# A decoder step's projection rewritten: token shift finished inside it, wider column chunks, zeros stored in seven pieces

## What is computed

```python
xn   = rmsnorm(x, g_mix)                       # x: 1088 rows of 1024
proj = xn @ w_in                               # 1024 x 3328
ret_p, rw_p = proj[..., :1536], proj[..., 1536:]
# token shift on the 1792 RWKV columns
prev = concatenate([s_shift, rw_p[:-1]])       # the row before; zeros / state_shift in front
rw_s = rw_p + (prev - rw_p) * rwkv_mu
s_shift_new = rw_p[:, -1]
```

## Time and profile before

| | before |
|---|---|
| median of three runs | 2183.63 us |
| the profiled execution | 2183.41 us, its span 2181.6 us |
| PE busy | 1847.1 us, 85% |
| DVE busy | 1217.1 us, 56% |
| ACT busy | 835.4 us, 38% |
| POOL busy | 305.9 us, 14% |
| projection, to the first instruction of the mixers | 0 to 365.0 us |
| mixers, to the first transfer of the attention | 365.0 to 885.1 us |

### The profile page before, as it was taken

The page is one execution under the profiler, slowest core; times in us unless marked ns, Lnnn a source line. Parts: engine busy times, 40 slices in busy tenths (PEclk is TensorE's granted clock), DMA queues, the critical chain, the costliest instruction groups (busy, mean ns, idle before and its releaser), DMA issues. The chain is left out here.

```text
span 2181.6 us, 36329 instructions
## 1 busy us (share of the span) xinstructions
PE 1847.1 (85%) x15218; PEld 1559.4 (71%) x15218; DVE 1217.1 (56%) x1285; ACT 835.4 (38%) x923; POOL 305.9 (14%) x262
## 2 busy tenths in 40 slices
PE   5999996687788879589999999854999999999940
PEld 5999996566666667478788888333888888888830
DVE  5200100776788876542333332127899999999926
ACT  4211210332333331340221212003777777777723
POOL 1000000322333323100000000001111111111003
PEclk9999998897999998799999999876999999999975
DMA  4422213417311120855201113526999999999928
GB/s 159 145 79 79 79 49 134 125 60 185 98 65 70 70 62 14 287 213 197 102 29 51 39 59 152 196 85 234 371 404 402 404 403 402 403 402 403 356 102 308
DMA packets 110630, 407.76 MB, mean 187 GB/s; under 512 B 25176, under 2 KB 47960, under 8 KB 82352
## 3 DMA queue, kind: packets, MB, share of 16 engines
q1 hardware_dynamic: 86000, 344.32, 42.6%
q10 hardware_dynamic: 17440, 36.00, 4.4%
q0 software_dynamic: 7072, 25.69, 3.0%
HBM read 345.91 MB, written 68.53 MB: 190 GB/s over the span
## 5 line engine op out<-in xcount | busy, mean ns | idle before, releaser
L2361 DVE TENSOR_TENSOR ex_w_lo<-moe_raw,ex_w_hi 128x2048 fp32r<-128x2048 f32 x192 | 431.2, 2285 | 67.0 <-ACT ex_w_hi L2426 66.9
L2426 ACT CAST ex_w_hi<-moe_raw 128x2048 fp32r<-128x2048 f32 x192 | 364.1, 1913 | 133.3 <-PE banks L2271 90.3
L2271 PE MATMUL banks<-ex_w_hi,ex_x_hi 128*128 128x512 f32 x512 | 208.0, 406 | 10.9 <-issue 6.4
L295 PE MATMUL banks<-pj_w_hi,pj_x_lo 128*128 128x416 f32 x576 | 203.7, 354 | 0.0
L295 PE MATMUL banks<-pj_w_hi,pj_x_hi 128*128 128x416 f32 x576 | 203.3, 353 | 0.1
L2271 PE MATMUL banks<-ex_w_hi,ex_x_lo 128*128 128x512 f32 x512 | 202.1, 395 | 0.0
L2271 PE MATMUL banks<-ex_w_lo,ex_x_hi 128*128 128x512 f32 x512 | 201.5, 394 | 0.0
L295 PE MATMUL banks<-pj_w_lo,pj_x_hi 128*128 128x416 f32 x576 | 201.5, 350 | 0.0
L199 DVE TENSOR_TENSOR pj_w_lo<-pj_w,pj_w_hi 128x3328 fp32r<-128x3328 f32 x8 | 29.0, 3623 | 221.6 <-ACT pj_w_hi L254 221.6
L247 ACT COPY pj_out<-banks 128x416 f32<-128x416 f32 x72 | 36.4, 506 | 253.7 <-PE banks L295 253.7
L2271 PEld LDWEIGHTS banks<-ex_w_hi,ex_x_hi 128*128 128x128 f32 x512 | 97.5, 190 | 42.9 <-issue 21.9
(11 more groups left out here) (375 smaller groups left out, 3823.4 us busy)
## 6 DMA issues: line engine op xcount, KB each, us to landing
moe_raw<-w_e_gate SPq DMA_DIRECT2D x64, 1024.0 KB, 7.7
moe_raw<-w_e_up SPq DMA_DIRECT2D x64, 1024.0 KB, 7.4
moe_raw<-w_e_down SPq DMA_DIRECT2D x64, 1024.0 KB, 7.4
blocks<-ex_y ACTq DMA_DIRECT2D x32, 512.0 KB, 7.7
proj<-pj_out ACTq DMA_DIRECT2D x72, 208.0 KB, 1.9
pj_w<-w_in SPq DMA_DIRECT2D x8, 1664.0 KB, 8.7
mx_pin<-proj SPq DMA_DIRECT2D x8, 1664.0 KB, 7.0
h<-at_h SPq DMA_DIRECT2D x18, 512.0 KB, 2.6
```

The source lines that it names most:

```text
L295: ins = pe.matmul(PS[:, 4 + t % BUFS, 0:W], a[:, t, k, :], b[:, par, k, :], start=k == 0 and n == 0, stop=k == KC - 1 and n == len(pairs) - 1)
L2271: ins = pe.matmul(out, a, b, start=first and i == 0, stop=final and i == 2)
L2361: v.tensor_tensor(w_lo[:, j], raw[:, j], as_f32(w_hi[:, j]), ALU.subtract).then_inc(S_("w_split"), 1)
L2426: act.copy(w_hi[:, j], raw[:, j]).then_inc(S_("w_high"), 1)
```

## The change

- **Inputs laid out on the host.** x comes turned as well (`xT`), w_in in column chunks whose every piece is one contiguous run in each partition, g_mix, state_shift and mu in the shapes of their tiles. No arithmetic moves to the host.
- **Projection.** 7 chunks instead of 8: four of 448 columns (the RWKV part, done first) and three of 512. The row norm is no longer applied to x but to the result, where PSUM is emptied; the gain g goes into the split of the weights. No PE transposes. The sample tile's low parts lie in the 64 unused columns of its high part, so it takes two matmuls a block instead of three. Banks go round over all eight.
- **Token shift in the projection.** For the RWKV chunks DVE writes from PSUM p = rstd·mu·(xW) to `pm` and rstd·(xW) − p to `out`; SP stores `pm` to DRAM one row down (`put`), reads the rows of the same tile back (`bring`), POOL adds them to `out`, SP stores that to `proj`. The new shift states are stored from here. 
- **Mixers.** No `prev`, no mu, no shift operations, no state_shift rows; `keys` and `key_sum` move forward on DVE; `load(j)` does not wait for r's shift; `lora_act` waits for the load.
- **Zeros.** Instead of 8 MB once, 2, 2, 2, 3, 2, 2 and 3 blocks of 512 KB, each behind the load of pairs 0 to 6.

The core of the diff:

```diff
+    CHUNKS = [(NRET + 448 * c, 448) for c in range(4)] + [(512 * c, 512) for c in range(3)]
+    NCH = len(CHUNKS)
+    shifted = lambda c: CHUNKS[c][0] >= NRET
+    W, HALF, BUFS, MB = 512, KC // 2, 5, 3
...
+                def load_w(c, h):
+                    i, n = 2 * c + h, HALF * CHUNKS[c][1]
+                    if i >= 3:
+                        sp.wait_ge(S_("w_split"), HALF * (i - 2))
+                    sp.dma_start(piece(c, h), d["w_in"][:, w_at[c] + h * n:w_at[c] + (h + 1) * n]).then_inc(S_(f"w_loaded{i % 3}"), 16)
...
+                def put(c, t):
+                    m, (col, n) = moved(c, t), CHUNKS[c]
+                    b, r = m % MB, rows_of(t)
+                    cols = slice(col - NRET, col - NRET + n)
+                    sp.wait_ge(S_("dve_evicted"), dve_evicted(c, t))
+                    sp.dma_start(d["pm"][t * P + 1:t * P + 1 + r, cols], pm[0:r, b, 0:n]).then_inc(S_(f"put{b}"), 16)
...
+                def bring(c, t):
+                    m, (col, n) = moved(c, t), CHUNKS[c]
+                    b, r = m % MB, rows_of(t)
+                    to, cols = S_(f"up{b}"), slice(col - NRET, col - NRET + n)
+                    sp.wait_ge(S_(f"put{b}"), 16 * (m // MB + 1))
+                    if m >= MB:
+                        sp.wait_ge(S_("added"), m - MB + 1)
+                    sp.dma_start(up[0:r, b, 0:n], d["pm"][t * P:t * P + r, cols]).then_inc(to, 16)
+                    if t == NT:
...
+                steps = [(c, t) for c in range(NCH) for t in range(TILES)]
+                for n in range(len(steps) + 2):
+                    if n < len(steps):
+                        c, t = steps[n]
+                        if t == 0 and 1 <= c < NCH - 1:
+                            load_w(c + 1, 0)
+                            load_w(c + 1, 1)
+                        if shifted(c):
+                            put(c, t)
+                    if 1 <= n <= N_SH * TILES:
+                        bring(*steps[n - 1])
+                    if n >= 2:
+                        store(*steps[n - 2])
...
+                def shares(c, t, src, cols):
+                    r, m, n = rows_of(t), moved(c, t), number(c, t)
+                    rstd, width = st[0:r, t, 2:3], CHUNKS[c][1]
+                    b = m % MB
+                    if m >= MB:
+                        v.wait_ge(S_(f"put{b}"), 16 * (m // MB))
+                    lk(v.scalar_tensor_tensor(pm[0:r, b, 0:width], src, rstd, mu[0:r, cols], ALU.mult, ALU.mult))
+                    if t >= NT - 1:
+                        q = slice(P - 32, P) if t < NT else slice(0, NS)
+                        if moved(c, t) > NT:
+                            v.wait_ge(S_("raw_stored"), 32 * (m // TILES))
+                        v.tensor_scalar(raw[q, 0:width], src[q], st[q, t, 2:3], None, ALU.mult)
+                    out_free(v, c, t)
+                    v.scalar_tensor_tensor(out[0:r, n % BUFS, 0:width], src, rstd, pm[0:r, b, 0:width], ALU.mult, ALU.subtract).then_inc(S_("dve_evicted"), 1)
...
+                        o = out[0:r, number(c, t) % BUFS, 0:width]
+                        po.wait_ge(S_("dve_evicted"), dve_evicted(c, t))
+                        po.wait_ge(S_(f"up{m % MB}"), 16 * ups(m, True))
+                        po.tensor_tensor(o, o, up[0:r, m % MB, 0:width], ALU.add).then_inc(S_("added"), 1)
...
+                def w_high(c, k):
+                    n, i = CHUNKS[c][1], 2 * c + k // HALF
+                    act.wait_ge(S_(f"w_loaded{i % 3}"), 16 * (i // 3 + 1))
+                    if c >= 2:
+                        act.wait_ge(S_("projected"), TILES * (c - 1))
+                    src = piece(c, k // HALF)[:, k % HALF * n:(k % HALF + 1) * n]
...
+                        terms = [(x_hi, w_hi), (x_hi, w_lo), (x_lo, w_hi)][0:3 if t < NT else 2]
+                        for k in range(KC):
+                            if t == 0:
+                                pe.wait_ge(S_("w_split"), KC * c + k + 1)
+                            for a, (xs, ws) in enumerate(terms):
+                                ins = pe.matmul(PS[:, n % 8, 0:width], xs[:, t, k, :], ws[:, c % 2, k, 0:width],
+                                                start=k == 0 and a == 0, stop=k == KC - 1 and a == len(terms) - 1)
+                        ins.then_inc(S_("projected"), 1)
...
-                        sp.wait_ge(S_("r_shifted"), j)
                         sp.wait_ge(S_("qk_ready"), j)
...
-                        sp.dma_start(pin[r, j % 2], d["proj"][j * P + 1:j * P + 1 + n, :]).then_inc(to, 16)
-                        sp.dma_start(prev[r], d["proj"][j * P:j * P + n, OR:NIN]).then_inc(to, 16)
+                        sp.dma_start(pin[r, j % 2], d["proj"][j * P:j * P + n, :]).then_inc(to, 16)
...
-                    if i == 1:
-                        sp.dma_start(d["blocks"][NE * P:NBLK * P, :], d["zero_row"][0:1, 0:D].broadcast_to([NOVER * P, D])).then_inc(S_("blocks_cleared"), 16)
-                sp.wait_ge(S_("loaded0"), 48 * (NT // 2) + 96)
-                for r in rows:
-                    sp.dma_start(prev[r.start:r.stop:DS, :], d["state_shift"][0]).then_inc(S_("shift_rows"), 16)
+                    lo, hi = NE + NOVER * i // (NT - 1), NE + NOVER * (i + 1) // (NT - 1)
+                    sp.dma_start(d["blocks"][lo * P:hi * P, :], d["zero_row"][0:1, 0:D].broadcast_to([(hi - lo) * P, D])).then_inc(S_("blocks_cleared"), 16)
                 store_ret(NT - 1)
...
                     if i >= 1:
                         y_center(i - 1)
                     level(i, 1)
-                    shift_v(j)
+                    keys(j)
                     level(i, 2)
-                    shift_k(j)
-                    keys(j)
+                    key_sum(j)
                     level(i, 3)
                     ret_sum(i)
                     turned_lora(j)
-                    key_sum(j)
                     level(i, 4)
                     rates(j)
                     if i >= 1:
                         y_sum(i - 1)
-                    shift_r(j)
                     level(i, 5)
                     key_norm(j)
                     ret_out(i)
...
-                    act.wait_ge(S_("v_shifted"), j + 1)
+                    act.wait_ge(S_(f"loaded{j % 2}"), loads_of(j))
...
```

More of the change, by code:

```diff
@@ new lines, in _ @@
+                x_high(1)
+                x_high(2)
+                square(0)
+                x_high(3)
+                square(1)
+                x_high(4)
+                x_high(5)
+                square(2)
+                x_high(6)
+                square(3)
+                x_high(7)
+                for k in range(HALF):
+                    w_high(1, k)
+                x_high(8)
+                for k in range(HALF, KC):
+                    w_high(1, k)
+                for t in range(4, TILES):
+                    square(t)
@@ L279, in _ @@
+                evict(0, NT)
+                for c in range(1, NCH):
+                    for t in range(TILES):
+                        if not shifted(c) or t == NT:
+                            evict(c, t)
+                        if c + 1 < NCH and t < KC:
+                            w_high(c + 1, t)
             @block.tensor
             def _(pe):
[L281 to L287 removed]
```

337 lines of the change are left out of this document (191 added, 146 removed).

## The result

| | before | after |
|---|---|---|
| median, the two measured beside each other | 2186.08 us (4 runs) | 2117.14 us (4 runs, 2114.5 to 2119.8) |
| the profiled execution | 2183.41 us, span 2181.6 | 2118.49 us, span 2116.7 |
| PE, DVE, POOL busy | 1847.1, 1217.1, 305.9 us | 1819.1, 1199.4, 342.5 us |

The ratio is 0.9688, with an interval of 0.9664 to 0.9711: 3.1% faster. The forecast was 2119.6 us in a range of 2095 to 2142.

What follows compares the result with a forecast made beforehand. PE was taken to bound the projection, and a ring between PE, DVE and ACT, no single engine, the mixers' pairs. Projection 35.3 plus mixers 28.5 us made 63.8 saved, 2183.4 to 2119.6 us, range 2095 to 2142.

Steps and rivals of the forecast that it cites:

- Projection, 35.3 us: Projection: matmuls save 17.1, chunk 0 10.8 and the start 8.9 us, the tail costs 1.5; 35.3 us saved.
- the 17.1 us for the matmuls: Projection: PE's matmuls fall from 326.2 to 309.1 us, at 0.2014 us for 448 columns and 0.2267 for 512.
- What must hide: Projection: work of DVE, POOL and SP per tile, some 15 us from PSUM to free buffer, hides behind PE; cost nothing.
- Rival (5): Projection: the ring through DRAM takes over three PE tiles (14.5 us), making the kernel slower, e.g. 2215.7 us; chance 0.02.
- Rival (4): Projection not fully hidden: DVE, slowed beside POOL, bounds 36 tiles by 0.55, 20 us, 2139.6 us; chance 0.06.
- Start and last pair, 6.5 and 5.6 us: Mixers: with prev and mu not loaded and shifts gone, the start saves 6.5 us and the last pair 5.6.
- Zeros, 15.0 us: Mixers: splitting the 8 MB of zeros, which cost pair 2 18.95 us, into seven pieces saves 15.0 us.
- the 0.6 us a piece: Mixers: each of the seven pieces of zeros was taken to cost 0.6 us, 4 in all.
- Rival (1): Mixers: the zeros cost as much in pieces as at once, 15 us more, 2134.6 us; chance 0.17.
- Steady pairs, 0.2 us each: Mixers: shifts removed save 0.35 + 1.03 us, key_sum's wait costs 1.2; net 0.2 us a pair, 1.4 in all.
- Rival (2): Mixers: key_sum's wait for ACT's square does not come, 9 us less, 2110.6 us; chance 0.08.
- rival (3): Mixers: DVE bounds the pairs and the shift comes off whole, 50.4 us instead of 1.4, 2070.6 us; chance 0.05.

Runs made afterwards that it cites:

- experiment 8: Changed kernel with 30 matmuls on a zeroed tile added ahead of the projection to warm PE; 2116.51 us.
- experiment 10: Changed kernel with the 1536 retention columns in four chunks of 384 instead of three of 512; 2117.86 us.
- experiment 11: Changed kernel with three output buffers in the projection instead of five; 2159.19 us.
- experiment 1: Kernel before the change, with only the zeros split into seven pieces; 2173.67 us against 2188.73, ratio 0.9939.
- experiment 3: Changed kernel with the 8 MB of zeros as one transfer again, behind the load of pair 1; 2137.08 us.
- experiment 6: Changed kernel with key_sum(j) put back behind level 3 of the solver; 2112.10 us, ratio 0.9677.
- experiment 4: Changed kernel with one more wait, so that POOL's rotary begins only after DVE has written the solver's first level; 2109.72 us.
- experiment 5: Changed kernel with an unread 896 KB load put where prev was, ahead of the rotary factors; 2131.83 us.
- experiment 7: Changed kernel with key_sum put back and POOL's rotary of tiles 2 to 8 behind level 1; 2105.91 us, ratio 0.9642.

## Why the forecast was right, and where it was not

The total was right to 2.5 us, and the mechanism of each large term held:

- *Projection, 35.3 us.* Measured 35.1. PE's start at 12.0 was 11.59; the 7.5 us for the first weights and a table load that was missing made up for each other; the steps were right to 0.002 us; the clock's start cost 14 steps by 0.17, 2.4 us, where 2.5 were taken, which experiment 8 gives back; no stop for a late instruction (1 taken); tail 1.9 against 1.5. Of the 17.1 us for the matmuls, the sample tile's 64 matmuls fewer are 12.1 us (64 by 0.1888) and the wider columns the rest; the forecast had not split these, and experiment 10 says that most of the value is in the first.
- *What must hide.* It did. Rival (5), the ring, was the sound one: a round is 13.7 to 14.3 us in experiment 11, where I had 15. That is nearly three tiles of PE, and the buffers beyond the third hide it. Rival (4) falls, since PE never waited.
- *Start and last pair, 6.5 and 5.6 us.* 8.0 and 6.3. The explanation by the missing load holds for the last pair (55.15 us with the load back, 55.41 before). For the start it is weaker: kernels with the same start ranged over 5 us, so 8.0 is no sharper than that.
- *Zeros, 15.0 us.* The step that failed is the 0.6 us a piece. The lump is worth 15.1 us in the time of experiment 1, 18.8 us in its pair before and 15.3 us in its pair in experiment 3; the pieces cost nothing that shows. Rival (1) falls.
- *Steady pairs, 0.2 us each.* The terms are right: 0.99 us off between levels 4 and 5, 0.97 us on for key_sum, and 0.3 off before level 2. Rival (2) falls with experiment 6, and rival (3), that the 7 us of DVE come off whole, with all of them. What failed is a step that was never made. I followed the removed load into the last pair and the start and not into the steady ones. There the transfers behind it land 2.2 us earlier, POOL starts earlier, and it now works beside two DVE operations that PE waits for. I had the row for it: 684 against 1755 ns for one operation, and used it for the projection only. PE's wait for these two is 0.8 us longer on the mean, and the pairs are 0.8 to 1.7 us longer with what PE's clock adds. That POOL has a part in it rests on experiments 4 and 5; how the gain divides between POOL and the clock stays open, since experiments 6 and 7 have equal pairs with and without the overlap.
- *Pair 1, 7.0 us.* Left out. In the trace of before PE waits 3.91 us at 472.67 for the rotary, whose rows come late behind `prev`:

```profile
472.67 0.90 PE L962 MATMUL banks<-mx_ident,mx_qk 128*128 128x128 f32 x4 [3.91 <-POOL mx_qk L723]
```

After, the same turning at 423.63 waits for nothing. Experiment 5 puts 3.5 us of the 7.0 back. The rest is within the scatter of the pair itself: in experiment 1, which has the same load and a wait of 4.11 us there, pair 1 takes 48.46 us and not 51.27.

The two large errors cancel: pair 1 and the zeros gave 10.6 us more than forecast (6.8 and 3.8), and the five steady pairs 9.7 us less in the first execution (8.7 longer instead of 1.0 shorter), some 5 in the second. The range would have held either alone, but the sum of pairs 1 to 6 was right partly by luck.

## What to carry to other kernels

When a load is taken away, follow the transfers that stood behind it: what lands earlier starts an engine earlier, and ask beside whose operations it then works. An engine far from being the bound (POOL, 16% busy) can make the ring's bound wait through a neighbour, and one wait that moves it behind those operations gave, together with `key_sum`'s old place, 11 us. Cut a long background transfer into pieces that end before the next load; seven of them cost nothing that showed, and the single one cost 15 to 19 us.

## What the runs showed of the hardware

- **GpSimd beside VectorE.** A DVE operation of 128x512 took 0.69 us alone and 0.87 to 1.26 us with POOL's rotary beside it, and one of POOL's 1.05 us instead of 0.72. Both lose. The Trainium skill (Trainium Architecture — The Big Picture, What this means for kernel authors) calls the ports that these two share an exclusive lock; the rows agree that they contend, and cannot tell a lock from a shared pace.
- **TensorE's clock in the mixers.** Of one kernel and the same instructions, the granted clock from load to level 1 was 0.57 on the mean in one pair and 0.78 in the next, and steady pairs of the unchanged kernel ranged from 48.7 to 51.2 us over two executions. With the waits set in another order (experiment 7) four pairs in a row agreed to 0.02 us.
- **The start.** PE idle until 11.59 us took 0.373 us a step for 13 steps (448 columns, so 1.2 GHz), PE busy with matmuls on zeros from 1.30 us took 0.20 from the second step on. The granted clock of the profile reads 1.00 in both.
- **A step's fixed part.** Steps of 384, 448 and 512 columns were 172.4, 201.6 and 225.1 ns; at 2.4 GHz the columns are 160.0, 186.7 and 213.3, so 12 to 15 ns are left (18 to 19 in the executions whose steps of 448 took 204.9 and 205.8). The Trainium skill (TensorE: Matmul & The Clock Gate, Back-to-back issue gap) gives N/2.4 plus 2.5 ns for an isolated matmul of N columns, 216 ns at 512, and about 131 ns at 512 for a sustained stream of weight loads and matmuls; these fp32r products took more than either.
- **Instructions under a long transfer.** PE stood 2.3 to 4.3 us for "issue", three or four times, under one transfer of 8 MB, both times with the end of the first stop 22 us after the transfer was issued. In the pairs of the changed kernel's two executions, with pieces of 1 to 1.5 MB, it never did. That it is instructions which wait for the queues is my reading of "issue"; no row shows it.
